# Stage order in three mixers and another front of the fourth in a fused four-mixer kernel

## The reference

```python
def fox_mixer(h, ...):                 # 16 heads of 64
    q, k, v, f, z = split(h @ w_in)    # f: 16 forget gates
    c = cumsum(log_sigmoid(f + b_f)); logits = q k^T * scale + c_q - c_k
    return (softmax(logits) @ v * silu(z)) @ w_out
def nsa_mixer(h, ...):                 # ks, vs, kw, vw, q, z projections of h
    kc = rope(silu(blocks(kc_raw) @ w_ck1) @ w_ck2)      # "hidden" tiles
    ...
def _hgrn2_mixer(h, ...):              # 8 heads, chunked gated recurrence
    o = rmsnorm(o, out_norm) * silu(g)
    return o @ w_out
def _mla_mixer(h, cos, sin, ...):      # 8 heads, 128 nope + 64 rope
    c_q, c_kv, k_rope = split(h @ w_in)
    q  = (rmsnorm(c_q, q_a_norm) @ w_q_up).reshape(B, S, 8, 192)
    kv = rmsnorm(c_kv, kv_a_norm) @ w_kv_up
    k = concat(k_nope, broadcast(k_rope))
    q = rope_tail(rmsnorm(q, q_norm)); k = rope_tail(rmsnorm(k, k_norm))
    return causal_softmax(q k^T / sqrt(192)) @ v @ w_out
```

## Time and profile before

| | |
|---|---|
| median of 3 runs | 1115.91 us |
| lowest and highest | 1108.06, 1118.05 us |
| the profiled execution | 1112.2 us |
| its span | 1110.4 us |
| mean granted TensorE clock | 0.984 |
| TensorE busy | 1058.5 us, 95% |
| VectorE, ScalarE, POOL busy | 69%, 49%, 7% |
| DMA | 152.31 MB, 137 GB/s |

### The profile page before, as it was taken

One profiled execution on the slowest core, in us unless ns is written; L12 is line 12 of the kernel. 1 busy time (PEld: TensorE's weight loads), 2 busy tenths in 40 slices (PEclk: granted clock), 3 DMA queues, 4 the chain that ended last, 5 costly groups with the idle time before them and its releaser, 6 DMA issues. The chain is left out here.

```text
span 1110.4 us, 20549 instructions
## 1 busy us (share of the span) xinstructions
PE 1058.5 (95%) x8304; PEld 993.9 (90%) x8306; DVE 770.7 (69%) x1276; ACT 548.7 (49%) x862; POOL 76.5 (7%) x60
## 2 busy tenths in 40 slices
PE   7999999999998999899999999999899899999997
PEld 5988889897676999898989999999888799999997
DVE  5666666767676667477456887787677548887875
ACT  5544445355555545543355544454564455544451
POOL 4000005000000410000011000000300320000000
PEclk9899999999999999999999999999999999999999
DMA  8544335782112446400345666664323045755641
GB/s 265 152 120 147 115 117 171 223 265 75 39 39 77 149 155 194 148 1 7 104 130 141 190 193 178 195 188 144 120 76 115 19 134 153 216 171 180 189 152 39
DMA packets 176974, 152.31 MB, mean 137 GB/s; under 512 B 6845, under 2 KB 169220, under 8 KB 176900
## 3 DMA queue, kind: packets, MB, share of 16 engines
q1 hardware_dynamic: 176690, 151.22, 45.0%
q10 hardware_dynamic: 210, 0.05, 0.0%
HBM read 148.12 MB, written 1.05 MB: 134 GB/s over the span
## 5 line engine op out<-in xcount | busy, mean ns | idle before, releaser
L421 PE MATMUL bank<-h_high,w_high 128*128 128x256 f32 x1312 | 381.9, 291 | 6.2 <-DVE ffn_normed L1040 2.6
L422 PE MATMUL bank<-h_low,w_high 128*128 128x256 f32 x1312 | 374.0, 285 | 0.0
L423 PE MATMUL bank<-h_high,w_low 128*128 128x256 f32 x1312 | 373.8, 285 | 0.0
L385 ACT ACTIVATE w_high<-ring 128x2048 fp32r<-128x2048 f32 x138 | 263.3, 1911 | 189.1 <-PE bank L423 181.9
L395 DVE TENSOR_TENSOR w_low<-ring,w_high 128x2048 fp32r<-128x2048 f32 x119 | 273.4, 2300 | 32.6 <-ACT w_high L385 32.4
L421 PEld LDWEIGHTS bank<-h_high,w_high 128*128 128x128 f32 x1312 | 254.4, 194 | 13.5 <-issue 8.3
L422 PEld LDWEIGHTS bank<-h_low,w_high 128*128 128x128 f32 x1312 | 254.6, 194 | 0.7 <-issue 0.5
L423 PEld LDWEIGHTS bank<-h_high,w_low 128*128 128x128 f32 x1312 | 254.5, 194 | 0.0
L421 PE MATMUL bank<-ffn_hidden_high,w_high 128*128 (+1 forms) x352 | 99.8, 283 | 2.0 <-DVE ffn_hidden_low L1073 2.0
L422 PE MATMUL bank<-ffn_hidden_low,w_high 128*128 (+1 forms) x352 | 99.6, 283 | 0.0
L423 PE MATMUL bank<-ffn_hidden_high,w_low 128*128 (+1 forms) x352 | 99.6, 283 | 0.0
(11 more groups left out here) (344 smaller groups left out, 1823.9 us busy)
## 6 DMA issues: line engine op xcount, KB each, us to landing
ring<-in_ffn_w_up_dram SPq DMA_DIRECT2D x44, 1024.0 KB, 6.0
ring<-in_ffn_w_down_dram SPq DMA_DIRECT2D x22, 1024.0 KB, 5.0
ring<-in_fox_w_in_dram SPq DMA_DIRECT2D x16, 1024.0 KB, 5.7
ring<-in_hgrn_w_in_dram SPq DMA_DIRECT2D x16, 1024.0 KB, 5.5
ring<-in_nsa_w_in_dram SPq DMA_DIRECT2D x14, 1024.0 KB, 5.4
ring<-in_fox_w_out_dram SPq DMA_DIRECT2D x4, 1024.0 KB, 5.1
ring<-in_nsa_w_out_dram SPq DMA_DIRECT2D x4, 1024.0 KB, 5.1
ring<-in_hgrn_w_out_dram SPq DMA_DIRECT2D x4, 1024.0 KB, 5.2
```

Of the source, the lines that this page charges most:

```text
L385: i = nc.scalar.activation(dst, src, ACT.Copy)
L421: nc.tensor.matmul(o, ah, bh, start=start, stop=False, **kw)
L422: nc.tensor.matmul(o, ah, bl, start=False, stop=False, **kw)
L423: return nc.tensor.matmul(o, al, bh, start=False, stop=stop, **kw)
```

## The change

- Fox: `forget_product` is cut into parts of 6, 5 and 5 matmuls, in the quarters 0, 1 and 2 of tile 1.
- `project_out`: its first tile is `by_feature_late`: chunks 0 to 5 of both halves, then chunks 6 and 7 of both.
- NSA: tile vw is used before hk0; VectorE makes its low part before `blocks(0)`.
- HGRN: unit 1's exponents go first and the evacuation is waited for after them; the Exp table is loaded before the last evacuation; each mixed level signals by itself; the first gate tile goes ahead of the last two heads' outputs; square sums and spreads are cut into pieces between the quarters of the gate tiles 1 and 2.
- FFN: the following norm's sums leave its block; in the fourth mixer VectorE adds the squares and `sums` is issued in the second input tile.
- MLA: c_q is split from its bank with its gain and without its row scale; the epsilon of q's norm is formed from c_q's own sums instead. The query is not scaled by its root: the minimum is multiplied by it and Exp gets the negative root as its scale. q_up's tiles are loaded with the rope part a second time, halves swapped (six transfers a tile), so that the product itself gives q and its turned form on 128 partitions, and one multiplication by a cosine-sine table does the turn; keys' rope is laid out twice to match. Queries need no spread, gain or rotation. Query squares are added on VectorE before they are summed. The last two keys' spreads and gains, the high part of two tiles and two half low parts move into attention.

```diff
+        def by_feature_late(pe, t, act, ready):
+            in_parts(pe, t)
+            wait_bank(pe, t)
+            w = parts(t, "p (c n) -> p c n", c=DC, n=256)
+            for chunks in (range(DC - 2), range(DC - 2, DC)):
+                for j in range(2):
+                    for c in chunks:
+                        if j == 0:
+                            ready(c)
+                        mm = product3(...)
+            mm.then_inc(tile_done, 1)
...
+            elif src[0] == "q_up":
+                dst = ring[:, t % NSLOT, :].rearrange("p (k e n) -> p k e n", k=2, n=256)
+                half = ROPE // 2
+                for k in range(2):
+                    w = src[1][:, k, 4 * src[2]:4 * src[2] + 4, :]
+                    sp.dma_start(dst[:, k, :, 0:QK], w).then_inc(q_swapped[src[2]] if k else s, 16)
+                    sp.dma_start(dst[:, k, :, QK:QK + half], w[:, :, QK - half:]).then_inc(q_swapped[src[2]], 16)
+                    sp.dma_start(dst[:, k, :, QK + half:], w[:, :, NOPE:QK - half]).then_inc(q_swapped[src[2]], 16)
...
                 def quarter(n, q):
                     if (n, q) == (1, 0):
                         nrm_fox.spread(pe)
+                    if n == 1 and q < 3:
+                        forget_product(q)
...
+                by_token(pe, NT2["vw"], hsp, between=rotate_after(1))
                 hidden("hk0", 0, 0)
-                by_token(pe, NT2["vw"], hsp, between=rotate_after(1))
...
                 low(dve, nc.vector, t_in + 4)
+                low(dve, nc.vector, t_in + 5)
                 dve.wait_ge(moved_x, 128)
...
                 for k in range(HG_H + 2):
                     if k < HG_H:
-                        exponents(2 * k)
-                        exponents(2 * k + 1)
+                        exponents(2 * k + (k == 0))
+                        exponents(2 * k + (k > 0))
...
+                    if k == HG_H:
+                        pe.wait_ge(decayed, NU)
+                        by_feature(pe, t_g, hsp)
                     if k >= 2:
                         outputs(k - 2)
...
+                by_feature(pe, t_g + 1, hsp, between=square_sums)
+                by_feature(pe, t_g + 2, hsp, between=spread_roots)
                 by_feature(pe, t_g + 3, hsp)
...
                     if following:
                         first_tile(pe)
-                        following.sums(pe)
...
                 by_feature(pe, t_mi + 1, hsp, between=in_tile)
+                evacuated(pe, t_mi)
+                for p in range(8):
+                    if p == 4:
+                        pe.wait_ge(lora_ready, 1)
+                    up(p)
                     if p == 0:
+                        rope_key()
+                        key_sums()
+                    if p == 1:
+                        rotate_key()
+                    if p >= 1:
                         sums(p - 1)
+                    if p >= 6:
                         spread_roots(p - 2)
                     if p in (5, 7):
                         up_values((p - 5) // 2)
+                sums(7)
...
+                for k in range(att5.steps):
+                    if k < 2:
+                        pe.wait_ge(root5, 7 + k)
...
+                    att5.pe_step(pe, k)
+                    if k < 2:
+                        spread_roots(6 + k)
...
+                nrm_mla.add_squares(dve, nc.vector)
+                for k in range(2):
+                    dve.wait_ge(cq_high, k + 1)
...
+                    i = nc.vector.scalar_tensor_tensor(out=c_lo[:, k, :], in0=bank2(t_mi)[:, k, :], scalar=pc("q_a", k),
+                                                       in1=c_hi[:, k, :].bitcast(F32), op0=ALU.mult, op1=ALU.subtract)
+                i.then_inc(freed(t_mi), 1)
                 low(dve, nc.vector, t_mq)
...
+                nrm_mla.finish(dve, meanwhile=angles)
...
+                nc.vector.tensor_tensor(w_r, w_r, bcast(pc("norm_mix", DC, DC), 2, P), ALU.mult).then_inc(w_r_ready, 1)
+                dve.wait_ge(tile_done, t_mi + 2)
+                nc.vector.tensor_tensor(ckv, bank2(t_mi + 1), row2, ALU.mult).then_inc(freed(t_mi + 1), 1)
...
+                for k in range(att5.steps):
+                    att5.act_step(act, k)
+                    if k in (3, 7):
+                        high(act, t_mkv + 3 + k // 7)
...
+                    att5.dve_step(dve, k)
+                    if k == 0:
+                        gain(7)
+                    if k in (6, 8):
+                        low_half(dve, t_mkv + 3, k // 2 - 3)
```

More of the change, by code:

```diff
@@ L335, in build @@
         T["mla_in"] = wtiles(mw, 0, 2 * LORA)
-        T["mla_q"] = wtiles(A["mla_w_q_up_2"][0], 0, ML_H * QK, step=4 * QK, kc=2)
+        T["mla_q"] = len(tiles)
+        tiles.extend(("q_up", A["mla_w_q_up_2"][0].rearrange("(c p) (h n) -> p c h n", p=P, n=QK), i) for i in range(2))
         T["mla_kv"] = wtiles(A["mla_w_kv_up_2"][0], 0, ML_H * 256, step=1024, kc=2)
@@ L350, in build @@
         bank_free = [sem(f"bank_free{i}") for i in range(2)]
+        q_swapped = [sem(f"q_up_swapped{i}") for i in range(2)]
         def load(sp, t):
@@ L380, in high @@
             landed(act, t, later)
+            if tiles[t][0] == "q_up":
+                act.wait_ge(q_swapped[tiles[t][2]], 80)
             if t >= NSLOT:
@@ L662, in __init__ @@
             def __init__(self, area, units, groups, take, blocks=None):
-                self.units, self.groups, self.take = units, groups, take
+                self.units, self.groups, self.take, self.step = units, groups, take, None
                 self.u0, self.g0, self.w0 = before["units"], before["groups"], before["weighs"]
@@ L895, in pe @@
             def pe(pe):
-                for t in range(t0, t0 + 4):
-                    by_feature(pe, t, split, ready=(lambda c: pe.wait_ge(act_split, n0 + c + 1)) if t == t0 else None)
+                by_feature_late(pe, t0, split, lambda c: pe.wait_ge(act_split, n0 + c + 1))
+                for t in range(t0 + 1, t0 + 4):
+                    by_feature(pe, t, split)
                 first(pe)
@@ L2415, in build @@
         oT = h
-        sqn, sqr, tcos, tsin = [area(2, 2, S) for _ in range(4)]
-        att_area = area.same(16 * S)
+        sqn, sqr = [area(2, 2, S) for _ in range(2)]
+        att_area = area
         rs2 = area(8, 4)
+        rs_minus = area(4, 4)
         t_mi, t_mq, t_mkv = T["mla_in"], T["mla_q"], T["mla_kv"]
@@ new lines, in rotate_key @@
+                def rotate_key():
+                    pe.wait_ge(kr_in, 2)
+                    nc.tensor.matmul(B[7][:, 0:S], C("rot2"), krg, start=True, stop=True).then_inc(lora_sum, 1)
+                    pe.wait_ge(lsq_in, 3)
+                    pe.wait_ge(ang_step, QUERY_EPS)
+                    for tt in range(TT):
+                        mm = nc.tensor.matmul(B[4][:, tt:tt + 1], kr_sq[0:ROPE, tt * P:(tt + 1) * P], ones[0:ROPE, 0:1],
+                                              start=True, stop=True)
@@ L2742, in _ @@
+                att5.step = lstep
+                for k in range(att5.steps):
+                    att5.dve_step(dve, k)
+                    if k == 0:
+                        gain(7)
+                    if k in (6, 8):
+                        low_half(dve, t_mkv + 3, k // 2 - 3)
                 out5_dve(dve)
```

462 lines of the change are left out of this document (251 added, 211 removed).

## The result

The changed kernel takes 1084.0 us (median of 6 runs, 1080.4 to 1086.5) against 1114.1 before: a ratio of 0.9738, 95% interval 0.970 to 0.9776. Its profiled execution took 1085.0 us around a span of 1083.2. First the busy times, then who waited for whom on TensorE (us in total, times, longest).

The account below looks back on a forecast made before the run. The prediction took TensorE's own queue to bound the kernel (busy 1058.5 of 1110.4 us). Its terms summed to 31.8 us, so 1112.2 - 31.8 = 1080.4, said as 1080, with a range of 1066 to 1096.

Parts of the forecast that it names:

- Forget product in thirds: Fox's forget product: cutting its row keeps the clock up, 26 slow records get 0.09 us back: 2.4 us.
- Late chunks: First tile of output projections: work put before the last chunks covers waits; fox 3.3, NSA 3.5, MLA 1.4 us.
- NSA order: NSA's start: vw before the first hidden tile saves a late low part and slow records; net 2.4 us.
- HGRN start: Start of hgrn: unit 1's exponents first, early Exp table, scores level by level; 2.2 us gained.
- HGRN end: Hgrn's tail: moved gate tile and cut sums and spreads gain 2.1 us, despite a 4.0 us wait for last chunks.
- Fourth mixer: Fourth mixer: work, waits and clock gain 21.7 us, new waits cost 7.2; net 14.5 us.
- Rival A: Inside attention, ScalarE and VectorE set the pace: 6.8 us more, 1087 us; chance 0.17.
- B: Rival, all the clock places: the clock gains don't come, 10.1 us missing, 1090 us; chance 0.10.
- C: Rival, fourth mixer and hgrn: new waits overestimated, 6.9 of 7.2 us vanish and 2 in hgrn, 1071 us; chance 0.12.
- D: Rival, q_up tile loads: the strips land late, holding products up by some 10 us, 1090 us; chance 0.04.
- E: Rival, fourth mixer: TensorE at the 1.2 GHz level throughout, about 45 us more, 1125 us; chance 0.02.
- F: Rival, weight pipeline: gives back what TensorE saves, half of the sum, 1096 us; chance 0.05.

Follow-up runs that it names:

- e9_forget_whole: The changed kernel with fox's forget product in one row of 16 matmuls again: 1085.5 us.
- e2_no_late: The changed kernel with the old order of chunks in the first tile of all four output projections: 1093.8 us.
- e10_same_again: The changed kernel executed again without any edit: 1082.5 us.
- e12_rows_repaired: TensorE's program of e3_old_tail with the VectorE and ScalarE queues of e4_tail_order: 1080.6 us.
- e4_tail_order: The changed kernel with another order on VectorE and ScalarE in hgrn's tail (gate tiles emptied once done, second output tile's low part last): 1076.7 us.
- e5_highs_out: The changed kernel with the two high parts of output-projection tiles moved out of attention on ScalarE: 1080.7 us (mean of two runs of four).
- e6_multiply_twice: The changed kernel with a second multiply (by 1.0) behind the one that scales each least logit in attention: 1083.3 us.
- best2: The changed kernel with all repairs: hgrn's tail order, c_kv's bank first, first two minima before last gains, attention free of weight tiles: 1072.4 us, ratio to before 0.9619.
- e8_start: The changed kernel with c_kv's bank emptied ahead of the rope weights' gain and attention's first two minima ahead of the last two gains: median 1080.4 us.
- e1_three_mixers: The kernel before with all of the change except the fourth mixer's own part: 1098.0 us, ratio to before 0.989.
- e3_old_tail: The changed kernel with hgrn's tail on TensorE as before (gate tile 0 behind the last heads, square sums and spreads in one row each): 1081.5 us.

## Why the prediction came out as it did

1080 was said and 1084.0 measured, inside the range (1066 to 1096). By steps:

- *Sum.* 21.7 at full clock and 10.1 of clock; 19.3 and 11.4 came. I had read the clock's share as seven stretches that are slow and will not be. The runs show that such a stretch comes and goes between executions at several places, and that the edits make it rarer (19.1 us lost to the clock in the mean before, 7.7 after). That the size held is in part luck: I read it from one profile, which happened to lose about as much (17.5 us, 1.6% of 1112.2) as the mean.
- *Range*: the bounds of the terms add up to 16.4 and 43.9 us, not to 20 and 46 as I wrote; the measured 30.0 (medians) lies inside either.
- *Forget product in thirds*: 2.4 said, 3.1 in the trace and 2.4 in the means. The cause, a row of thin records that brings the half clock, is shown by `e9_forget_whole`.
- *Late chunks*: waits 7.7 said and 6.5 measured by `e2_no_late`, clock 2.6 and 3.8 (good to 1.9). Right for the waits; for the clock the size is within the error, so that my bound "waits alone" is unlikely and not refuted.
- *NSA order*: 2.4 and 2.4, with the new wait for `kw` at 1.32 (1.2 said). Read from the traces alone; no run takes it apart.
- *HGRN start*: 2.2 and 2.1 in the traces.
- *HGRN end*: the step that was mis-sized. I said 2.1. The mechanism was seen, and the 4.0 us wait forecast (3.7), but I credited 2.1 to the whole stage without asking what the late chunks give with the old tail: they alone take that wait from 2.6 to 0.5. The new tail by itself costs 3.8 us at full clock and gives 2.6 in clock, -1.2 in all. With the 2.1 of the late chunks the stage is worth about 0.9 in the means; the -1.5 of the table holds the square sums at 0.57, which were at 1.00 in `e10_same_again`. With the queues mended it costs nothing at full clock and gives 4.5 in clock (`e12_rows_repaired` against `e4_tail_order`).
- *Fourth mixer*: 14.5 with 1.0 of clock, so 13.5, and 12.2 measured. Front 21.2 said and 21.8 found, in the traces; no run takes the front apart into squares, spreads, rotations and waits. Inside attention 2.5 was said and the waits grew by 3.6 (from 1.6 to 5.2). What fills them: 1.4 by the two high parts (`e5_highs_out`); a second multiply in each unit adds nothing (`e6_multiply_twice`); `best2` is 2.3 us shorter there than `e5_highs_out` and holds both the start (1.4 by `e8_start`) and the low halves, so some 0.9 is left for these, by subtraction. The rest, 1.3 of the 3.6, stays open.
- *Rival A* (ScalarE and VectorE pace attention): a sixth came true, 1.1 of 6.8. *B* (no clock gains): refuted, 11.4 came where I had 10.1. *C* (new waits overestimated): they were 7.8 against 7.2, so no. *D*: see below. *E* (1.2 GHz through the fourth mixer): its front was granted 1.00. *F* (the weight pipeline gives it back): refuted by `e1_three_mixers`; weight tiles stood in the way in hgrn's tail and in attention, by the order of the queues, and a late low part held up the start of hgrn.

**Rival D**, the 128-byte strips. Transfers in the changed kernel (queue, count, KB each, median us to landing):

```profile
ring<-in_mla_w_q_up_dram SPq DMA_DIRECT2D x4, 384.0 KB, 3.8
...
ring<-in_mla_w_q_up_dram SPq DMA_DIRECT2D x8, 64.0 KB, 3.6
```

The single transfers land in 3.6 to 3.8 us (medians), but a whole tile, six of them in a row, is there 6.4 and 6.6 us after its first issue (756.71 to 763.15 and 767.66 to 774.22), where one plain load took 4.4. So the strips cost some 2 us a tile in landing and none in time: the second tile's high part starts at 781.55, 14 us after its issue. The Trainium skill ("DMA: Bandwidth & Descriptors", Specifications) says that pieces under 512 bytes lose line rate; the trace agrees in direction, since 64 KB in strips of 128 bytes take about as long as 384 KB in pieces of 768.

## What to carry to other kernels

Compare variants by time times mean granted clock beside the time: it told edits of 1.6 and 4.4 us apart where the times of one kernel scatter by 4 to 19. When an engine is made to arrive earlier, follow the in-order queues of the others and ask of each item who wants it first; in hgrn's tail and in attention, weight tiles that were wanted 2 to 27 us later stood ahead of what TensorE waited for. All repairs of the order together brought another 11 us, 8.5 of them at full clock and 4.4 of these in hgrn's tail. And cost an edit of a pair against the kernel that has the other one already.

## What the runs showed of the hardware that I had not expected

- Slow stretches come and go between executions of one kernel: 518 to 526 us was granted 0.57 in one and 1.00 in the next. The instructions before it were the same, and so was the one short wait (0.56 us). The Trainium skill ("TensorE: Matmul & The Clock Gate", What's actually happening) says that the chip's observation of activity runs free and does not start anew with the kernel. The traces fit that and don't prove it: `e3_old_tail` reaches the start of hgrn 0.3 us earlier than the changed kernel (380.95 against 381.28) with the same work before it, and is granted full clock there.
- Cutting two rows of 32 thin records into pieces between full-width work, with one gate tile moved, costs nothing at full clock (1071.1 both ways) and saves 4.5 us of clock in the mean.
- The clock falls inside attention too, where 136 of 168 records have 128 columns and not the products' 256: 31.7 us at 1.00 in four profiles, 32.2 to 33.4 at 0.95 in five, with the same code of attention but for one multiply in one of the five.
- A low part of a weight tile takes 2.28 us, and 2.92 where a POOL cast of 1.48 us starts 0.7 us ahead of it.
